# A product-key expert layer: three instead of two token blocks by gathered rows, one-hots made four tokens at a time, expert names resolved in batches

## Chip, cores and metric

One core of a Trainium2 chip. The metric is the device time of one execution in microseconds (us), median of several runs. The engines are TensorE (PE; its weight loads are PEld), VectorE (DVE), ScalarE (ACT), GpSimd (POOL) and SyncE (SP, here only a DMA queue).

## The reference

A decoder layer on 1024 tokens of width 1024. Its first half (projections, retention and window attention, layer norm) is untouched by the change. The second is an expert FFN whose experts are single neurons:

```python
q = (xt @ w_pq).reshape(T, 8, 2, 128)
s = einsum('thpd,hpkd->thpk', q, sub_keys)            # 2 x 128 scores per head
s1, i1 = top_k(s[:, :, 0], 16); s2, i2 = top_k(s[:, :, 1], 16)
cand = s1[..., :, None] + s2[..., None, :]            # 256 pairs
top_s, pos = top_k(cand, 16)                          # idx = i1 * 128 + i2 of the pair
g = softmax(top_s)                                    # 8 heads x 16 experts a token
a = gelu(x . u_tab[idx]) * g                          # 16384 experts in all
y = sum over the 128 chosen of a * v_tab[idx]
h = layer_norm(ALPHA * h + y)
```

## The kernel before

Five stages follow one another, each a block that all engines leave together: `project`, `attend`, `score`, `experts_in` and `experts_out`. Tokens lie in TB = 8 blocks of 128.

**Two ways to the same sum.** For the first GB = 2 token blocks each chosen row is gathered: an indirect DMA on GpSimd's queue fetches for 128 tokens one row of 1024 numbers each (512 KB), 128 gathers a block. For the other DB = 6 blocks all 16384 experts are computed densely (DT = 768 tokens), as 128 slices of 128 experts, and a matrix of gates, zero where an expert isn't chosen, selects.

**`score`** computes scores head by head (a turn for each of PH = 8 heads) and stores those of blocks 1 to 7. Beside it VectorE does the top-k of token block 0: `side` twice (top 16 of 128), `pairs` (top 16 of 256), `gaps`, and, one turn later, `names` (which expert each of the 16 places means, by a compare with 0..15, a product and a sum) and `gates` (the softmax), which needs `exp` of ScalarE.

**`experts_in`** runs eight blocks s = 0..7 of four turns q; a turn has eight steps n, numbered m = 4s + q. In each step TensorE does half an expert slice: z = u . h for half of the dense tokens, 24 matmuls (three for each of eight pieces of the width, the operands being split in a high and a low part, `u_hi` by ScalarE, `u_lo` by GpSimd, line 787). ScalarE copies z out and stores it. From s = GB on, TensorE also builds the gates matrix of token block s: four matmuls a step, one for each token, of two one-hot matrices, `hot2` (line 1211) and `hot1_g` (line 1213, one-hot times gate). VectorE's order in a step is `make_hot`, a piece of the top-k of token block s + 1 (piece n % 4: two sides, pairs, names), and one `dot` (line 1222) of a gathered row of u with the token's own h, from a ring of four row buffers. GpSimd's order in a step is `u_lo` (every second step) and one gather, which waits until its ring slot is used. TensorE, in order, does a half slice, then waits for the one-hots of the step before. The semaphores are `hot_in` (one-hots ready), `row_here` and `row_used` (ring), `z_done`, `u_hi_in`, `u_lo_in`.

**`experts_out`** runs NG = 32 rounds of four slices over the dense token blocks. Each step of a round is one token block: ScalarE's gelu, VectorE's product with the gates (line 1442), ScalarE's `a_hi`, VectorE's `a_lo` (line 1447), 24 matmuls of 512 columns with v (lines 1346 to 1348), and VectorE's two additions of the sums to y (line 1455). Between these VectorE adds gathered rows of v to y for the gathered blocks (`add_row`, line 1434), 256 in all over the first 31 rounds, again through a ring of four (`RING`); `added` frees a slot. GpSimd splits v (`v_lo`, line 1397, four a round, each behind ScalarE's `v_hi`) and issues the gathers between (line 1387). `finish` is the last layer norm of a token block.

Of the kernel before, what the change touches and what calls it, by code (L numbers as in the profile page):

```python
# [33 lines left out]
GB = 2  # L34
# [213 lines left out]
class Ahead:  # L248
# [5 lines left out]
    def __init__(self, nc, ctx):  # L254
# [4 lines left out]
        self.g_in = self.carve(DT // GT, GROUP * GT)  # L259
        self.v_raw = [self.carve(D) for _ in range(2)]  # L260
# [5 lines left out]
        self.wq_raw = [self.carve(KT, P) for _ in range(2)]  # L266
        self.wq_here = [sem(f"wq_here{p}") for p in range(2)]
# [432 lines left out]
class TopK:  # L700


    def __init__(self, nc, ctx):
        sb = memory(nc, ctx)[0]
        self.nc = nc
        self.places = sb("places", [P, TOPK])
        self.s_cp, self.s_left = sb("s_cp", [P, 2, NK]), sb("s_left", [P, 2, NK])
        self.top, self.top_f = sb("top", [P, 2, TOPK]), sb("top_f", [P, 2, TOPK])
        self.top_i = sb("top_i", [P, 2, TOPK], U32)
        self.cand, self.cand_left = sb("cand", [P, TOPK, TOPK]), sb("cand_left", [P, TOPK * TOPK])  # L710
        self.best, self.pos = sb("best", [P, TOPK]), sb("pos", [P, TOPK], U32)
        self.ab, self.ab_f = sb("ab", [P, 2, TOPK], U32), sb("ab_f", [P, 2, TOPK])
        self.pick = sb("pick", [P, 2, TOPK, TOPK])
        self.gap, self.gap_e = sb("gap", [P, TOPK]), sb("gap_e", [P, TOPK])
        self.gap_sum, self.gap_r = sb("gap_sum", [P, 1]), sb("gap_r", [P, 1])
        self.found = sb("found", [P, 3, PH, TOPK])
# [10 lines left out]
    def side(self, link, p):  # L727

        self.top16(link, self.s_cp[:, p], self.s_left[:, p], self.top[:, p], self.top_i[:, p])

    def pairs(self, link):
# [3 lines left out]
        self.top16(link, self.cand[:].rearrange("p a b -> p (a b)"), self.cand_left[:], self.best, self.pos)  # L735

    def gaps(self):

        return self.nc.vector.tensor_scalar(self.gap[:], self.best[:], self.best[:, 0:1], None, ALU.subtract)

    def names(self, link, h):
# [3 lines left out]
        nc.vector.tensor_copy(self.top_f[:], self.top_i[:])  # L745
        nc.vector.tensor_scalar(self.ab[:, 0], self.pos[:], 4, None, ALU.logical_shift_right)
        link(nc.vector.tensor_scalar(self.ab[:, 1], self.pos[:], 15, None, ALU.bitwise_and))
        link(nc.vector.tensor_copy(self.ab_f[:], self.ab[:]))
        link(nc.vector.tensor_tensor(self.pick[:], bc(self.ab_f[:], 3, TOPK),
                                     bc(bc(self.places[:], 1, TOPK), 1, 2), ALU.is_equal))  # L750
        link(nc.vector.tensor_tensor(self.pick[:], self.pick[:], bc(self.top_f[:], 2, TOPK), ALU.mult))
        link(nc.vector.tensor_reduce(self.found[:, 0:2, bass.ds(h, 1), :].rearrange("p a h k -> p a (h k)"),
                                     self.pick[:], AX.X, ALU.add))

    def exp(self):

        return self.nc.scalar.activation(self.gap_e[:], self.gap[:], ACT.Exp, accum_out=self.gap_sum[:])

    def gates(self, link, h):
        nc = self.nc  # L760
        link(nc.vector.reciprocal(self.gap_r[:], self.gap_sum[:]))
        link(nc.vector.tensor_scalar(self.found[:, 2, bass.ds(h, 1), :].rearrange("p h k -> p (h k)"),
                                     self.gap_e[:], self.gap_r[:], None, ALU.mult))
# [27 lines left out]
def score(nc, d, hT_hi, hT_lo, tk, tiles, ahead):  # L791
# [3 lines left out]
    with ExitStack() as ctx:  # L795
# [18 lines left out]
        with nc.Block() as block:  # L814
# [56 lines left out]
            def _(act):  # L871
# [17 lines left out]
                def turn(h):  # L889
                    last = isinstance(h, int) and h == PH - 1  # L890
                    query(h, 0)
                    if not (isinstance(h, int) and h == 0):
                        act.wait_ge(gaps, h)
                        tk.exp().then_inc(exps, 1)
# [18 lines left out]
                act.wait_ge(gaps, PH)  # L913
# [9 lines left out]
            def _(v):  # L923
# [18 lines left out]
                def finish_top(h):  # L942

                    tk.names(link, h)
                    v.wait_ge(exps, h + 1)
                    tk.gates(link, h)

                def turn(h):
                    last = isinstance(h, int) and h == PH - 1
# [3 lines left out]
                    if not (isinstance(h, int) and h == 0):  # L953
                        finish_top(h - 1)
# [8 lines left out]
                    tk.side(link, 0)  # L963
                    tk.side(link, 1)
                    tk.pairs(link)
                    tk.gaps().then_inc(gaps, 1)
# [5 lines left out]
                turns(v, PH, turn)  # L972
                finish_top(PH - 1)


def experts_in(nc, d, hT_hi, hT_lo, tk, tiles, ahead):
# [7 lines left out]
    RING = 4  # L984
    PER_TURN = GB * PH * TOPK // TB
    with ExitStack() as ctx:
# [6 lines left out]
        hot2 = [sb(f"hot2_{g}", [P, 4, NK]) for g in range(2)]  # L993
        hot1_g = [sb(f"hot1_g{g}", [P, 4, NK]) for g in range(2)]
        g_sb = [sb(f"g_sb{b}", [P, NK, GT]) for b in range(2)]
        rows_in = ahead.rows + [sb(f"u_rows{i}", [P, D]) for i in range(RING - len(ahead.rows))]
        h_own = sb("h_own", [P, GB, D])
        z_ps = [[bank(f"z_ps{e}{a}") for a in range(2)] for e in range(2)]
        g_ps = [ctx.enter_context(nc.psum_tensor(f"g_ps{g}", [P, 4, NK], F32)) for g in range(2)]
        product = ctx.enter_context(nc.psum_tensor("product", [P, D], F32))  # L1000
# [8 lines left out]
        hot_in = [sem(f"hot_in{g}") for g in range(2)]  # L1009
        g_done = [sem(f"g_done{g}") for g in range(2)]  # L1010
# [564 lines left out]
```

## Time and profile before

| | |
|---|---|
| median of 3 runs | 3459.11 us (3454.69 to 3463.78) |
| the profiled execution | 3475.62 us, span 3474.0 us |
| busy in the span: PE, DVE, ACT, POOL | 3085.9, 2711.0, 987.2, 1418.4 us |
| mean granted clock of TensorE | 0.953 |
| `project`, `attend`, `score` | 0 to 747.8 us |
| `experts_in` | 747.8 to 2321 us |
| handing over | 2321 to 2366 us |
| `experts_out` | 2366 to 3474 us |

Busy is time in which an engine executes; waits don't count. A window of the span divides this by stage, and the difference between its length and an engine's busy time is that engine's idle time. Instructions of one engine overlap at their ends, so the distance between two starts, not the length, is what one costs. An instruction that is held up by another engine's use of memory is shown as a long one, not as idle time.

### The profile page before, as it was taken

What the parts mean: (1) busy time and instruction counts of PE and PEld (TensorE: products, weight loads), DVE (VectorE), ACT (ScalarE), POOL (GpSimd) and SP (SyncE); (2) the same over time, 40 slices, a digit from 0 to 9 for tenths busy, and PEclk for the clock granted to TensorE, in tenths of its full rate; (3) what the DMA queues carried; (4) which work ended last, traced back from release to release, by engine and by line L of the source; (5) the groups of instructions that cost most, each with busy time, mean ns of one, the idle gap of its engine ahead of it and who ended that gap; (6) DMA issues with size and microseconds to landing.
All of it is one profiled execution on the core that took longest, in us unless ns stands there. A gap on an engine that the chain in (4) does not pass through costs nothing. (4 is left out here: it accounts for less than half of the span.)

```text
span 3474.0 us, 43072 instructions
## 1 busy us (share of the span) xinstructions
PE 3085.9 (89%) x15866; PEld 2757.8 (79%) x15866; DVE 2711.0 (78%) x5430; ACT 987.2 (28%) x1565; POOL 1418.4 (41%) x878
## 2 busy tenths in 40 slices
PE   8997989989987888888888888866999999999997
PEld 6886877879887888787878888865787888787886
DVE  4125764559999989989899897546888898888889
ACT  2103331112222332333323333332332333333331
POOL 4113210025543333333333333335665656566563
PEclk9998999999998999999999999988999999999999
DMA  4214222336654554554555545658888788787873
GB/s 163 98 61 151 90 72 82 98 115 210 217 206 174 202 191 177 202 204 174 214 190 188 207 176 208 228 193 284 298 283 302 266 284 289 266 296 270 295 272 115
DMA packets 294042, 695.59 MB, mean 200 GB/s; under 512 B 20448, under 2 KB 136544, under 8 KB 290656
## 3 DMA queue, kind: packets, MB, share of 16 engines
q1 hardware_dynamic: 190944, 316.66, 27.8%
q0 software_dynamic: 73728, 268.47, 20.9%
q10 hardware_dynamic: 29184, 108.01, 7.9%
q8 instruction: 113, 1.85, 0.2%
q14 instruction: 73, 0.60, 0.0%
HBM read 565.13 MB, written 127.93 MB: 200 GB/s over the span
## 5 line engine op out<-in xcount | busy, mean ns | idle before, releaser
L787 POOL TENSOR_TENSOR u_lo<-u_raw,u_hi 128x1024 fp32r<-128x1024 f32 x128 | 321.6, 2512 | 1116.9 <-ACT u_hi L783 1116.7
L1062 PE MATMUL z_ps<-hT_hi,u_hi 128*128 128x384 f32 x2048 | 728.0, 355 | 35.2 <-POOL u_lo L787 23.8
L1063 PE MATMUL z_ps<-hT_lo,u_hi 128*128 128x384 f32 x2048 | 709.2, 346 | 0.0
L1064 PE MATMUL z_ps<-hT_hi,u_lo 128*128 128x384 f32 x2048 | 707.4, 345 | 0.0
L1346 PE MATMUL y_ps<-v_hi,a_hi 128*128 128x512 f32 x1536 | 603.8, 393 | 70.4 <-DVE a_lo L1447 45.0
L1347 PE MATMUL y_ps<-v_lo,a_hi 128*128 128x512 f32 x1536 | 601.2, 391 | 0.0
L1348 PE MATMUL y_ps<-v_hi,a_lo 128*128 128x512 f32 x1536 | 600.7, 391 | 0.0
L1397 POOL TENSOR_TENSOR v_lo<-room,v_hi 128x1024 fp32r<-128x1024 f32 x128 | 344.2, 2690 | 248.8 <-ACT v_hi L1374 247.1
L1062 PEld LDWEIGHTS z_ps<-hT_hi,u_hi 128*128 128x128 f32 x2048 | 406.4, 198 | 39.6 <-POOL u_lo L787 28.0
L1072 PE MATMUL g_ps<-hot_g,hot 128*128 128x128 f32 x1536 | 232.9, 299 | 193.8 <-DVE hot_g L1213 193.8
L1063 PEld LDWEIGHTS z_ps<-hT_lo,u_hi 128*128 128x128 f32 x2048 | 404.8, 198 | 0.0
L1064 PEld LDWEIGHTS z_ps<-hT_hi,u_lo 128*128 128x128 f32 x2048 | 403.0, 197 | 0.0
L1346 PEld LDWEIGHTS y_ps<-v_hi,a_hi 128*128 128x128 f32 x1536 | 290.1, 189 | 142.1 <-DVE a_lo L1447 45.2
L1072 PEld LDWEIGHTS g_ps<-hot_g,hot 128*128 128x128 f32 x1536 | 210.4, 207 | 219.9 <-DVE hot_g L1213 219.9
L1348 PEld LDWEIGHTS y_ps<-v_hi,a_lo 128*128 128x128 f32 x1536 | 290.4, 189 | 61.0
L1347 PEld LDWEIGHTS y_ps<-v_lo,a_hi 128*128 128x128 f32 x1536 | 290.3, 189 | 59.6
L1129 ACT ACTIVATE z_sb<-z_ps 128x384 f32<-128x384 f32 x256 | 124.7, 490 | 700.5 <-PE z_ps L1064 700.5
L1213 DVE TENSOR_SCALAR hot_g<-iota,iT,gT 128x128 f32<-128x128 f32 x768 | 320.5, 482 | 0.0
L1434 DVE SCALAR_TENSOR_TENSOR y<-v_rows,a_rows,y 128x1024 f32<-128x1024 f32 x192 | 277.8, 1468 | 29.0 <-DMA v_rows<-in_v,room 28.9
L1387 POOL DMA_INDIRECT v_rows<-in_v,room x192 | 238.7, 1243 | 135.2 <-DVE y L1434 102.4
L1115 ACT ACTIVATE g_sb<-g_ps 128x512 f32<-128x512 f32 x192 | 212.3, 1106 | 261.1 <-PE g_ps L1072 261.1
L1222 DVE CUSTOM_DVE_ANT_0 product<-u_rows,h_own 128x1024 f32<-128x1024 f32 x192 | 244.7, 1274 | 40.0 <-DMA u_rows<-in_u,room 35.4
(184 smaller groups left out, 5010.4 us busy)
## 6 DMA issues: line engine op xcount, KB each, us to landing
u_raw<-in_uT SPq DMA_DIRECT2D x128, 512.0 KB, 3.6
room<-in_v SPq DMA_DIRECT2D x128, 512.0 KB, 6.7
z<-z_sb ACTq DMA_DIRECT2D x128, 384.0 KB, 2.6
gates<-g_sb ACTq DMA_DIRECT2D x24, 2048.0 KB, 7.9
z_in<-z SPq DMA_DIRECT2D x16, 1536.0 KB, 12.7
g_in<-gates SPq DMA_DIRECT2D x16, 1536.0 KB, 19.5
room<-z SPq DMA_DIRECT2D x15, 1536.0 KB, 12.2
room<-gates SPq DMA_DIRECT2D x15, 1536.0 KB, 20.3
```

Source lines behind the costliest of these rows:

```text
L787: self.nc.gpsimd.tensor_tensor(self.u_lo[e][:], self.u_raw[e][:], self.u_hi[e][:].bitcast(F32), ALU.subtract).then_inc(self.u_lo_in[e], 1)
L1062: nc.tensor.matmul(o, u_hi[e][:, k], hT_hi[:, k, cols], start=(k == 0), stop=False)
L1063: nc.tensor.matmul(o, u_hi[e][:, k], hT_lo[:, k, cols], start=False, stop=False)
L1064: last = nc.tensor.matmul(o, u_lo[e][:, k], hT_hi[:, k, cols], start=False, stop=(k == KT - 1))
L1072: last = nc.tensor.matmul(g_ps[g][:, t], hot2[g][:, t], hot1_g[g][:, t], start=True, stop=True)
L1213: last = nc.vector.tensor_scalar(hot1_g[g][:, t], iota[:], iT[:, 0, t0 + t:t0 + t + 1], gT[:, t0 + t:t0 + t + 1], ALU.is_equal, ALU.mult)
L1222: nc.vector.tensor_tensor_reduce(product[:], rows_in[r][:], h_own[:, b], 1.0, 0.0, ALU.mult, ALU.add, ahead.z_rows[:, b, slot:slot + 1]).t ...
L1346: nc.tensor.matmul(o, ah, v_hi[p][:, i, c], start=(i == 0), stop=False)
L1347: nc.tensor.matmul(o, ah, v_lo[p][:, i, c], start=False, stop=False)
L1348: last = nc.tensor.matmul(o, al, v_hi[p][:, i, c], start=False, stop=(i == GROUP - 1))
L1397: nc.gpsimd.tensor_tensor(v_lo[r % 2][:, i], v_raw[i % 2][:], v_hi[r % 2][:, i].bitcast(F32), ALU.subtract).then_inc(v_lo_in[i % 2], 1)
L1434: nc.vector.scalar_tensor_tensor(y[:, b], rows_in[i % RING][:], a_rows[:, b, slot:slot + 1], y[:, b], ALU.mult, ALU.add).then_inc(added[b], 1)
```

## The change

GB goes from 2 to 3: 384 instead of 256 rows are gathered in either expert stage, the dense part has 5 token blocks (640 tokens, matmuls of 320 columns in `experts_in`, five steps a round in `experts_out`), and the gates matrix begins at s = 3. In `experts_in` dots are spread unevenly over the blocks, the ring has three slots, and h is loaded a token block at a time into two buffers. Both one-hots are plain compares for four tokens at once, with 0..127 read from a copy in PSUM (`iota_ps`); ScalarE multiplies one of them by the gates. `names` and `gates` are no longer done head by head, but for four and for eight heads; the top-k reads the loaded scores without a copy. The out stage's code is unchanged but for GB.

```diff
-GB = 2
+GB = 3
@@ class TopK
-    def names(self, link, h):
+    def names(self, link, half):
         nc = self.nc
-        nc.vector.tensor_copy(self.top_f[:], self.top_i[:])
...
-        link(nc.vector.tensor_copy(self.ab_f[:], self.ab[:]))
...
+        hs = slice(half * PH // 2, (half + 1) * PH // 2)
+        nc.vector.tensor_scalar(self.ab[:, 0], self.pos[:, hs], 4, None, ALU.logical_shift_right)
+        link(nc.vector.tensor_scalar(self.ab[:, 1], self.pos[:, hs], 15, None, ALU.bitwise_and))
+        link(nc.vector.tensor_tensor(self.pick[:], bc(self.ab[:].rearrange("p a h k -> p a (h k)"), 3, TOPK),
+                                     bc(bc(self.places[:], 1, PH // 2 * TOPK), 1, 2), ALU.is_equal))
+        for a in range(2):
+            last = nc.vector.tensor_tensor(...)
+        link(last)
+        link(nc.vector.tensor_reduce(...))
@@ score, VectorE: behind the last head
-                turns(v, PH, turn)
-                finish_top(PH - 1)
+                for h in range(PH):
+                    turn(h)
+                tk.gaps().then_inc(gaps, 1)
+                for half in range(2):
+                    tk.names(link, half)
+                v.wait_ge(exps, 1)
+                tk.gates(link)
@@ experts_in
-    RING = 4
-    PER_TURN = GB * PH * TOPK // TB
+    RING = 3
+    PER_TURN = [48, 48, 48, 46, 46, 46, 46, 56]
...
+        def own_rows(s, q, n):
+            before, k = sum(PER_TURN[:s]), q * 8 + n
+            return range(before + PER_TURN[s] * k // 32, before + PER_TURN[s] * (k + 1) // 32)
@@ SyncE
-                sp.dma_start(h_own[:], d["h"].rearrange("n p c -> p n c")[:, 0:GB]).then_inc(h_here, 16)
+                for b in range(2):
+                    sp.dma_start(h_own[b][:], d["h"][b]).then_inc(h_here[b], 16)
                 for m in range(Q * TB):
+                    done = own_rows(m // Q, m % Q, 0).start // (PH * TOPK)
+                    if done > (...) and done + 1 < GB:
+                        sp.wait_ge(row_used, done * PH * TOPK)
+                        sp.dma_start(h_own[(done + 1) % 2][:], d["h"][done + 1]).then_inc(...)
@@ ScalarE
+                def scale_hot(gm, n):
+                    g, t0 = n % 2, gm % Q * GT + 4 * n
+                    act.wait_ge(hot_in[g], 4 * gm + n // 2 + 1)
+                    for t in range(4):
+                        last = nc.scalar.activation(hot1_g[g][:, t], hot1[g][:, t], ACT.Copy,
+                                                    scale=gT[:, t0 + t:t0 + t + 1])
+                    last.then_inc(hot_g_in[g], 1)
...
                             if s >= GB:
+                                scale_hot(gm, n)
                                 if n:
                                     take_gates(gm, n - 1)
@@ GpSimd
-                            gather(s * PER_TURN + q * 8 + n)
+                            for i in own_rows(s, q, n):
+                                gather(i)
@@ VectorE
+                link(nc.vector.tensor_copy(iota_ps, iota[:]))
...
+                def top_piece(s, q, n):
+                    m, j, piece = s * Q + q, n // 3, n % 3
+                    if j < 2:
...
+                    elif n == 6 and q % 2:
+                        tk.names(link, q // 2)
+                    elif n == 7 and q == Q - 1:
+                        v.wait_ge(exps, s + 1)
+                        tk.gates(link)
...
-                    nc.vector.tensor_tensor(hot2[g][:], bc(iota[:], 1, 4), bc(iT[:, 1, t0:t0 + 4], 2, NK), ALU.is_equal)
-                    for t in range(4):
-                        last = nc.vector.tensor_scalar(hot1_g[g][:, t], iota[:], iT[:, 0, t0 + t:t0 + t + 1],
-                                                       gT[:, t0 + t:t0 + t + 1], ALU.is_equal, ALU.mult)
+                    for hot, side in ((hot2, 1), (hot1, 0)):
+                        last = nc.vector.tensor_tensor(hot[g][:], bc(iota_ps, 1, 4), bc(iT[:, side, t0:t0 + 4], 2, NK),
+                                                       ALU.is_equal)
...
-                            dot(s * PER_TURN + q * 8 + n)
+                            for i in own_rows(s, q, n):
+                                dot(i)
```

VectorE's order in one step of `experts_in` where both kinds of work run (names: `hot` a one-hot, `room`, `u_rows` row buffers, `near` the PSUM copy of 0..127; ISA rows with h_own are the dots), before:

```order
L1211 TENSOR_TENSOR hot_0<-iota,iT 128x512
L1213 TENSOR_SCALAR hot_g<-iota,iT,gT 128x128 x4
L734 TENSOR_TENSOR cand<-top 128x256
L721 MAX best<-cand 128x8
L722 MAX_INDEX pos<-best,cand 128x8
L723 MATCH_REPLACE cand_left<-best,cand 128x256
L724 MAX best<-cand_left 128x8
L725 MAX_INDEX pos<-best,cand_left 128x8
L739 TENSOR_SCALAR gap<-best 128x16
L1222 ISA product,room<-u_rows,h_own 128x1024
```

and now:

```order
L1242 TENSOR_TENSOR hot_0<-near,iT 128x512 x2
L738 TENSOR_TENSOR room<-top 128x256
L725 MAX best<-room 128x8
L726 MAX_INDEX pos<-best,room 128x8
L727 MATCH_REPLACE room<-best,room 128x256
L728 MAX best<-room 128x8
L729 MAX_INDEX pos<-best,room 128x8
L1253 ISA u_rows,room<-u_rows,h_own 128x1024
L1253 ISA room 128x1
L1253 ISA room<-room,h_own 128x1024
```

Five one-hot instructions have become two, and every second step has a second dot.

GpSimd's order in a round of `experts_out` (gathers into `v_rows` or, for one ring slot, `room`), before:

```order
L1397 TENSOR_TENSOR v_lo<-room,v_hi 128x1024
L1387 DMA v_rows<-in_v,room 128x1024 x2
L1397 TENSOR_TENSOR v_lo<-room,v_hi 128x1024
L1387 DMA v_rows<-in_v,room 128x1024
L1387 DMA room<-in_v,room 128x1024
L1387 DMA v_rows<-in_v,room 128x1024
L1397 TENSOR_TENSOR v_lo<-room,v_hi 128x1024
L1387 DMA v_rows<-in_v,room 128x1024 x2
```

and now:

```order
L1429 TENSOR_TENSOR v_lo<-room,v_hi 128x1024
L1419 DMA v_rows<-in_v,room 128x1024
L1419 DMA room<-in_v,room 128x1024
L1419 DMA v_rows<-in_v,room 128x1024
L1429 TENSOR_TENSOR v_lo<-room,v_hi 128x1024
L1419 DMA v_rows<-in_v,room 128x1024 x2
L1419 DMA room<-in_v,room 128x1024
L1419 DMA v_rows<-in_v,room 128x1024
L1429 TENSOR_TENSOR v_lo<-room,v_hi 128x1024
```

Mostly two gathers stood between two splits of v; now there are three or four.

## Rows read from the trace of the kernel before

**Rows 1.** Windows by stage: us, busy (x count) per engine, granted clock, DMA share, GB/s.

```profile
747.80:913.00 165.20, 153.93 (x845) 152.04 (x846) 148.29 (x356) 36.51 (x69) 87.75 (x53) 0.96 0.65 221
913.00:1066.60 153.60, 130.28 (x721) 127.72 (x720) 146.38 (x355) 30.94 (x61) 76.58 (x47) 0.95 0.60 207
1066.60:1279.00 212.40, 181.97 (x1028) 178.30 (x1027) 193.58 (x514) 66.28 (x96) 73.66 (x47) 0.91 0.49 178
2131.40:2321.00 189.60, 166.37 (x996) 163.87 (x996) 111.66 (x226) 60.90 (x77) 71.16 (x45) 0.95 0.59 220
2401.00:3401.00 1000.00, 979.01 (x4268) 801.95 (x4267) 868.96 (x957) 324.10 (x472) 614.97 (x360) 0.99 0.83 285
```

**Rows 2.** VectorE by line, 1066.6 to 2131.4: count, busy us, mean ns, idle before it.

```profile
L1213 DVE TENSOR_SCALAR hot_g<-iota,iT,gT 128x128 f32<-128x128 f32 x640 | 276.7, 497 | 0.0
L1211 DVE TENSOR_TENSOR hot<-iota,iT 128x512 f32<-128x512 f32 x160 | 157.9, 987 | 0.2
...
L1222 DVE CUSTOM_DVE_ANT_0 product<-room,h_own 128x1024 f32<-128x1024 f32 x40 | 49.3, 1233 | 43.7 <-issue 42.9
```

**Rows 3.** VectorE's timeline in block 3: start us, length us, instruction.

```profile
1291.71 1.23 DVE L1222 CUSTOM_DVE_ANT_0 product<-u_rows,h_own 128x1024 f32<-128x1024 f32 x1
...
1292.87 0.69 DVE L1211 TENSOR_TENSOR hot<-iota,iT 128x512 f32<-128x512 f32 x1
1293.47 1.11 DVE L1213 TENSOR_SCALAR hot_g<-iota,iT,gT 128x128 f32<-128x128 f32 x4
1294.50 0.42 DVE L734 TENSOR_TENSOR cand<-top 128x256 f32<-128x256 f32 x1
```

**Rows 4.** VectorE by line, 747.8 to 1066.6 (blocks 0 and 1).

```profile
L762 DVE TENSOR_SCALAR found<-gap_e,gap_r 128x16 f32<-128x16 f32 x16 | 37.0, 2314 | 0.6
L748 DVE CAST ab_f<-ab 128x32 f32<-128x32 uint32 x16 | 31.2, 1948 | 0.5
```

**Rows 5.** VectorE's timeline at the end of the scoring stage, last head.

```profile
737.09 0.28 DVE L961 TENSOR_SCALAR s_cp<-s_out 128x256 f32<-128x256 f32 x1
737.42 0.29 DVE L721 MAX8 top<-s_cp 128x8 f32<-128x128 f32 x1
...
743.86 0.23 DVE L739 TENSOR_SCALAR gap<-best 128x16 f32<-128x16 f32 x1
...
746.95 0.23 DVE L762 TENSOR_SCALAR found<-gap_e,gap_r 128x16 f32<-128x16 f32 x1
```

**Rows 6.** VectorE by line, 2401 to 3401 (out rounds).

```profile
L1434 DVE SCALAR_TENSOR_TENSOR y<-v_rows,a_rows,y 128x1024 f32<-128x1024 f32 x184 | 265.6, 1465 | 20.6 <-DMA v_rows<-in_v,room 20.5
...
L1447 DVE TENSOR_TENSOR a_lo<-room,a_hi 128x512 fp32r<-128x512 f32 x89 | 105.7, 1187 | 0.0
...
L1434 DVE SCALAR_TENSOR_TENSOR y<-room,a_rows,y 128x1024 f32<-128x1024 f32 x61 | 85.0, 1393 | 110.4 <-DMA room<-in_v,room 110.4
```

**Rows 7.** VectorE's timeline, one step of an out round.

```profile
2723.05 1.27 DVE L1455 TENSOR_TENSOR y<-y_ps,y 128x512 f32<-128x512 f32 x2
2724.25 0.67 DVE L1447 TENSOR_TENSOR a_lo<-room,a_hi 128x512 fp32r<-128x512 f32 x1
2724.85 1.27 DVE L1434 SCALAR_TENSOR_TENSOR y<-v_rows,a_rows,y 128x1024 f32<-128x1024 f32 x1
2726.05 0.67 DVE L1442 TENSOR_TENSOR room<-room 128x512 f32<-128x512 f32 x1
```

**Rows 8.** Source view of line 1455: ns min/median/max, first and last start.

```profile
L1455 DVE TENSOR_TENSOR y<-y_ps,y x384: 668/676/687, 2386.9 to 3465.4; 128x512 f32<-128x512 f32 x192
```

**Rows 9.** VectorE by line, 2131.4 to 2321 (block 7).

```profile
L1222 DVE CUSTOM_DVE_ANT_0 product<-room,h_own 128x1024 f32<-128x1024 f32 x8 | 11.3, 1412 | 51.0 <-DMA room<-in_u,room 51.0
```

**Rows 10.** TensorE's timeline in an out round.

```profile
2724.39 0.39 PE L1346 MATMUL y_ps<-v_hi,a_hi 128*128 128x512 f32 x1
2724.62 0.39 PE L1347 MATMUL y_ps<-v_lo,a_hi 128*128 128x512 f32 x1
```

**Rows 11.** DMA issues, 2401 to 3401: count, median us to landing.

```profile
v_rows<-in_v,room POOLq DMA_INDIRECT x183, 8.2
```

More of the change, by code:

```diff
@@ L700, with __init__ @@
 class TopK:
-    def __init__(self, nc, ctx):
+    def __init__(self, nc, ctx, room):
         sb = memory(nc, ctx)[0]
@@ L940, in scores @@
                                           s_ps[p][1][:].rearrange("p (t k) -> p t k", k=NK)).then_inc(s_dve, 1)
[L942 to L946, printed above, removed]
                 def turn(h):
-                    last = isinstance(h, int) and h == PH - 1
+                    last = h == PH - 1
                     query(h, 0)
@@ L962, in turn @@
                     nc.vector.engine_nop().then_inc(s_taken, 1)
[L963 to L966, printed above, removed]
+                    for p in range(2):
+                        tk.side(link, p, h, tk.s_cp[:, p])
+                    tk.pairs(link, h)
                     chain.restart()
@@ L993, in experts_in @@
         hot2 = [sb(f"hot2_{g}", [P, 4, NK]) for g in range(2)]
+        hot1 = [sb(f"hot1_{g}", [P, 4, NK]) for g in range(2)]
         hot1_g = [sb(f"hot1_g{g}", [P, 4, NK]) for g in range(2)]
@@ L996, in experts_in @@
         rows_in = ahead.rows + [sb(f"u_rows{i}", [P, D]) for i in range(RING - len(ahead.rows))]
-        h_own = sb("h_own", [P, GB, D])
+        h_own = [sb(f"h_own{b}", [P, D]) for b in range(2)]
         z_ps = [[bank(f"z_ps{e}{a}") for a in range(2)] for e in range(2)]
         g_ps = [ctx.enter_context(nc.psum_tensor(f"g_ps{g}", [P, 4, NK], F32)) for g in range(2)]
-        product = ctx.enter_context(nc.psum_tensor("product", [P, D], F32))
+        near = ctx.enter_context(nc.psum_tensor("near", [P, 512], F32))
+        iota_ps, iT_ps, gT_ps = near[:, 0:NK], near[:, P:3 * P].rearrange("p (a t) -> p a t", a=2), near[:, 3 * P:]
         const_here, u_here, u_hi_in, u_lo_in = tiles.const_here, tiles.u_here, tiles.u_hi_in, tiles.u_lo_in
@@ L1009, in experts_in @@
         hot_in = [sem(f"hot_in{g}") for g in range(2)]
+        hot_g_in = [sem(f"hot_g_in{g}") for g in range(2)]
         g_done = [sem(f"g_done{g}") for g in range(2)]
@@ L1012, in experts_in @@
         g_stored = [sem(f"g_stored{b}") for b in range(2)]
-        picked_in, h_here = sem("picked_in"), sem("h_own_here")
+        picked_in, h_here = sem("picked_in"), [sem(f"h_own_here{b}") for b in range(2)]
         row_here = [sem(f"u_row_here{i}") for i in range(RING)]
@@ L1491, in build @@
             attend(nc, d, hT_hi, hT_lo, ahead, spent)
-            tk = TopK(nc, inner)
+            tk = TopK(nc, inner, ahead)
             tiles = ExpertTiles(nc, inner)
```

100 lines of the change are left out of this document (49 added, 51 removed).

## The prediction

> **What bounds the kernel now.** I read the windows first, stage by stage, then the costs by line inside them, then the timeline for the distance from one start to the next. The "in" stage is eight blocks of 16 expert slices. Blocks 0 and 1 take 165 and 154 us, blocks 2 to 6 take 212 to 213 us each (five alike, the first stands there), block 7 takes 190 us; then come 32 "out" rounds, of which a stretch of 1000 us is shown [rows 1]. The reader is to see which engine is full: VectorE is busy 148 of 165, 146 of 154 and 194 of 212 us, and the granted clock there is 0.91 to 0.96, so TensorE, though busy, pauses. In the out rounds TensorE is busy 979 of 1000 us. So the in stage is paced by VectorE (block 7 less clearly, 112 of 190) and the out stage by TensorE.
>
> The second thing to see is how much of VectorE's time is a standstill. In blocks 2 to 6 the group of one-hot instructions on line 1213 has a mean of 497 ns and line 1211 of 987 [rows 2], while the same instructions undisturbed start 0.60 (line 1211) and 1.03 us for all four (line 1213) before the next [rows 3]. Over five blocks, 640 x (497-340) + 160 x (987-690) ns is 148 us (340 for one of the four: 1.11 less three starts of 0.257), 30 us a block; with 44 us of unexplained idle before the dots [rows 2] that is about 40 us a block. In blocks 0 and 1 it is line 762 (2314 ns for 16 elements, 230 elsewhere) and the cast of line 748 (1948 ns for 32 elements), together about 31 us a block [rows 4, 5].
>
> **Change, part 1: the end of the scoring stage.** Per head, the two sides and the pairs run from 737.42 to 743.86, 6.4 us, and the names and gates until 747.18, 3.3 us [rows 5]. The latter now leaves the turns, where TensorE hides it, and comes once behind the last head, where nothing hides it since all engines wait for the block's end. Price of a batched piece: 512 elements take 0.67 us and 1024 take 1.27 [rows 7], so 1.15 ns an element and about 2.45 us for 2048. One half is two shifts (0.3), a compare (2.45), two products of 1024 (2.5) and a sum (2.45): 7.7 us. Two halves are 15.4, plus 0.9 for the gates, against 3.3 now: **+13 us**.
>
> **Part 2: blocks 0 to 2 (no gates matrix now in block 2 either).** VectorE per block, undisturbed: top-k 8 x 6.4 = 51 plus 15.4 + 1.3 = 67 us (now 8 x 10.1 = 81), and 48 dots of 1.16 us [rows 3] = 56 us (now 37). That is 123 us against 118. On top there are about 41 us of standstill now. The two worst offenders shrink from eight times a block to a few, but more dots stand beside the same 16 u_lo instructions; I keep 31 (bounds 10 and 45). 154 us a block. TensorE needs less than now, since each matmul has 320 columns for 384; ScalarE and GpSimd are far from full. Three blocks: 462 against 165 + 154 + 212 = 531, **-69 us**.
>
> **Part 3: blocks 3 to 6.** One-hots: two compares of 0.60 us for 32 turns = 38 us, for 32 x 1.63 = 52 now. Top-k 67 for 81. Dots 46 x 1.16 = 53 for 37. Sum 158.5 against 170. The real gain is the standstill of 43 us: the 30 us that lie in the one-hots should go, because their first operand now lies in PSUM. The nearest row is the addition of line 1455, of the same size with one operand in PSUM: 384 of them lie between 668 and 687 ns [rows 8], while line 1447, of the same size with both in SBUF, has a mean of 1187 beside the same GpSimd work [rows 6]. The Trainium skill, SBUF — State Buffer, section "Who interferes with whom", has this as a rule: VectorE and GpSimd share one port pair as an exclusive lock, and an instruction with at most one SBUF input outside the two-port modes does not contend. By that rule, the trace agrees. I leave 17 us around the 46 dots and 4 us of waits for the transposes: 180 us (bounds 167, with hardly any standstill, and 202, with all of it). ScalarE gets four scalings a turn; at the 0.26 us of one of VectorE's [rows 3] that is 33 us on top of 66 of 212 [rows 1]: off the path. What is moved: SP's load of h_own is split in three with one wait for row_used ahead of it, in front of u loads that are needed a turn later; I cost it at nothing. Four blocks: **-132 us**.
>
> **Part 4: block 7.** No top-k, but 56 dots for 32. Here VectorE is idle 78 us, almost all of it in front of dots: 51 us for one ring slot alone [rows 9]. The order explains it: a gather stands behind u_lo on GpSimd's queue, this waits for u_hi on ScalarE, this for matmuls, and these for one-hots that stand behind the dot. The loop gets 0.4 us a turn shorter by the one-hots and longer by the scaling and a second dot. I take 176 for 190, **-14 us** (bounds 155 and 200).
>
> In stage in all: **-215 us**.
>
> **Part 5: the out rounds.** Matmuls start 0.23 us apart [rows 10], 979/4268 = 0.229 in the stretch [rows 1]: 144 a round are 33.0 us, 120 are 27.5. If TensorE stayed the bound, 32 rounds would give back 176 us. VectorE decides against it. 245 row additions in 1000 us at 256/31 = 8.26 a round make a round of 33.7 us; VectorE is busy 869 and the remaining 131 us are all waits for a gathered row [rows 1, 6]. Starts inside one undisturbed step: two additions 1.20, a_lo 0.60, row 1.20 us [rows 7]. With the mean stretch of rows 6 (rows 1.447 against 1.27, a_lo 1.187 against 0.68) a round now has 8.26 x 1.38 = 11.4, 12 x 0.60 = 7.2, 6 x 1.11 = 6.7, and the remainder of the 29.3 busy, 4.0, for six products. After: 384/31 = 12.39 rows x 1.38 = 17.1, 10 additions 6.0, 5 a_lo 5.5, 5 products 3.3: 31.9 us busy, above TensorE's 27.5. The waits for rows are 4.4 us a round now, and slack, since TensorE is full; once VectorE is the bound they are on the path. Do they go away? A slot comes free with its addition, and the gather into it takes 8.2 us to land [rows 11]; four slots at 12.39 rows in T us need a turnaround of T/3.1. At T = 36.7 that is 11.8 us: 8.2 to land, 1.2 the addition, and 2.4 us for GpSimd, which may be in a v_lo of 2.4 us or waiting for v_hi with the gathers behind it, and for VectorE's other steps. I take waits of 4.8 us, T = 36.7 (bounds 31.9, no waits, and 41). 31 rounds x 3.0 = +93, the last round, without rows, -6: **+87 us**.
>
> **Sum:** 13 - 69 - 132 - 14 + 87 = -115 us. On the profiled execution, 3475.6, that is 3361; it lay 16 us over the median of 3459.1, so the forecast is **3344 us**.
>
> **Rivals.**
> 1. *Rows land in time.* The gathers are issued early enough and only the 31.9 us stay: 31 x (-1.8) - 6 = -62 in place of +87, so 3195 us. For it: once TensorE has time to spare, ScalarE's v_hi and GpSimd's v_lo come earlier, and the gathers behind them. Against it: turnaround would have to be 10.3 us, hardly more than landing plus addition. 14%.
> 2. *The ring decides (slower than before).* One mechanism in the out rounds: four slots, three rows for each v_lo, and each slot's cycle is 8.2 + 1.2 + 3.8 = 13.2 us, a round of 13.2 x 3.1 = 40.9, +223 - 6. The same in the in stage, where the ring shrinks to three: 10.5 us a cycle is 3.5 a row, 168 a block in blocks 0 to 2 (-27) and 196 in block 7 (+6), blocks 3 to 6 unchanged. Sum 13 - 27 - 132 + 6 + 217 = +77: 3536 us. It makes the kernel slower from about 12.4 us on in the out stage, if the in stage suffers too, and from 13 if not. For it: the waits are there already, with 8.26 rows. Against: now the gathers also wait because TensorE is slow. 14%.
> 3. *The one-hots still stand still* (the change doesn't do what it should): the 30 us stay in blocks 3 to 6 and most in block 7, +145: 3489 us. Line 1455 speaks against it. 6%.
>
> Another is inside the forecast: TensorE, with 27 us of work in a round of 37, pauses in each step. In block 2, at 182 us busy in 212, the granted clock was still 0.91 [rows 1]; only under 0.75 would the matmuls need the whole round. The Trainium skill, TensorE: Matmul & The Clock Gate, Part 1, has the engine fall to 1.2 GHz after idling; were that so throughout, 54 us a round would be needed and the kernel far slower. The row of the in blocks says pauses of this kind cost a tenth.
>
> **How the numbers follow.** Forecast 66%, rivals 14, 14 and 6. A measurement of this kernel can tell about 0.3%, 10 us, from no change. Faster: nearly all of the forecast and rival 1, 0.79. Slower: most of rivals 2 and 3, 0.16. Within 0.3%: what of each falls about the old time, 0.05. The range 3220 to 3500 takes in the forecast's bounds (in stage -260 to -130, out stage +20 to +160, not all at one end), rival 3 and the nearer halves of rivals 1 and 2.
>
> **What would show it.** VectorE's one-hots near 0.68 us without a tail; blocks 3 to 6 at about 180 us, blocks 0 to 2 at about 154; the in stage beginning some 13 us later behind the last scores; TensorE's busy share in the out rounds about 75% with VectorE's idle time all before row additions; a round of about 36.7 us. I am wrong if rounds get shorter than 33 us or longer than 40, or if blocks 3 to 6 stay above 200.

## The result and the profile after

The changed kernel takes **3862.45 us** (median of 4 runs, 3857.36 to 3866.29) against 3459.48 (4 runs, 3454.69 to 3463.78): a ratio of 1.1164, 95% interval 1.1144 to 1.1185. That is 403 us slower where 115 us less were forecast, and far outside the range. The profiled span is 3855.6 us, the mean granted clock 0.867 (before 3474.0 and 0.953).

First the stages: blocks 0, 1 and 2, then a stretch of one block's length among blocks 3 to 6, block 7 with the end of the stage, and 1140 us of out rounds, as in [rows 1]. This is the windows view of the changed kernel; columns are the stretch, its length, then the busy time (and number) of PE, PEld, VectorE, ScalarE and GpSimd, the granted clock, the DMA share and GB/s.

```profile
761.00:935.00 174.00, 143.08 (x862) 139.95 (x863) 142.73 (x317) 34.31 (x54) 106.57 (x67) 0.91 0.74 248
935.00:1101.40 166.40, 128.89 (x763) 125.21 (x763) 146.07 (x314) 31.01 (x49) 104.00 (x65) 0.90 0.73 240
1101.40:1276.70 175.30, 117.05 (x711) 113.48 (x710) 143.21 (x316) 28.85 (x46) 102.02 (x65) 0.87 0.70 230
1535.00:1800.00 265.00, 171.08 (x1026) 166.26 (x1026) 163.70 (x374) 96.89 (x209) 92.82 (x64) 0.81 0.51 179
2320.40:2563.00 242.60, 168.90 (x1000) 164.69 (x998) 106.06 (x177) 94.57 (x206) 90.87 (x71) 0.83 0.62 220
2640.00:3780.00 1140.00, 880.88 (x3530) 708.37 (x3529) 1016.39 (x959) 284.44 (x412) 783.50 (x485) 0.87 0.86 293
```

In the fourth row no engine is full. VectorE is busy 163.7 of 265 us, close to the 158.5 that the prediction added up, and the block lasts 265 all the same. TensorE is busy 171. With no engine full and the DMA share down at 0.51, waits must set the pace, and one looks for a chain of waits that comes back to its start, a circle.

Measured between the same marks in both kernels, in us. The in stage starts with its first matmul; blocks are divided where VectorE starts on a block (block 0 is counted from the start of the stage, block 7 to its last matmul); an out round is the time from the first row addition to the last, divided by 31:

| | in stage starts | blocks 0, 1, 2 | blocks 3 to 6 | block 7 | out round |
|---|---|---|---|---|---|
| before | 747.9 | 165 154 213 | 215 212 211 214 | 188 | 33.5 |
| forecast | +13 | 154 154 154 | 180 each | 176 | 36.7 |
| after | 761.0 | 174 167 175 | 258 265 260 260 | 236 | 38.2 |

By spans: +13 before the in stage, +229 in it (1802.0 for 1573.2), -4 in the handing over, +143 in the out stage (1251.6 for 1108): 381.

The waits of blocks 3 to 6 in the changed kernel name the links of the circle (columns: who waited, for whom, us in total, how often, longest).

```profile
POOL u_lo L794 <- ACT u_hi L790: 630.6, 64, 12.9
ACT hot_g L1129 <- DVE hot L1242: 555.7, 116, 17.3
...
PE g_ps L1087 <- ACT hot_g L1129: 352.6, 76, 10.2
DVE u_rows L1253 <- issue: 132.8, 23, 10.0
DVE u_rows L1253 <- DMA u_rows<-in_u,room: 123.8, 30, 7.6
```

GpSimd waits 631 of 1043 us for u_hi, 64 times, which is every time, and ScalarE 556 us for one-hots. The first of these alone shows nothing new: in blocks 3 to 6 of the kernel before (852 us) it was there as well, with the same count and nearly the same share of the time:

```profile
POOL u_lo L787 <- ACT u_hi L783: 522.2, 64, 12.8
```

There ScalarE waited for TensorE (361 us for z, 181 for the gates matrix) and 47 us for VectorE's gaps, never for one-hots. Its wait for VectorE's one-hots is the new link. One turn of the circle, in the timeline of the changed kernel in block 4 (start, duration, engine, line, operation, in brackets the idle time before it):

```profile
1597.76 1.06 ACT L790 ACTIVATE u_hi<-u_raw 128x1024 fp32r<-128x1024 f32 x1
...
1598.90 2.39 POOL L794 TENSOR_TENSOR u_lo<-u_raw,u_hi 128x1024 fp32r<-128x1024 f32 x1 [12.38 <-ACT u_hi L790]
...
1601.44 0.96 POOL L1188 DMA_INDIRECT room<-in_u,room  x1
...
1602.29 1.27 ACT L1129 ACTIVATE hot_g<-hot,gT 128x128 f32<-128x128 f32 x4
...
1607.22 1.23 DVE L1253 CUSTOM_DVE_ANT_0 room<-room,h_own 128x1024 f32<-128x1024 f32 x1 [9.88 <-issue]
...
1608.37 1.28 DVE L1242 TENSOR_TENSOR hot<-near,iT 128x512 f32<-128x512 f32 x2
...
1609.69 0.40 ACT L1129 ACTIVATE hot_g<-hot,gT 128x128 f32<-128x128 f32 x1 [3.78 <-DVE hot L1242]
...
1610.87 1.06 ACT L1139 ACTIVATE g_sb<-g_ps 128x512 f32<-128x512 f32 x1
...
1611.71 1.07 ACT L790 ACTIVATE u_hi<-u_raw 128x1024 fp32r<-128x1024 f32 x1
```

The circle runs from u_hi to GpSimd's u_lo; behind it on GpSimd's queue stands the gather, 5.8 us before its dot starts; behind the dot on VectorE's queue come the next step's one-hots; ScalarE's scaling waits for these, and behind the scaling on ScalarE's queue stands the next u_hi. From u_hi to u_hi is 13.95 us here; a block has 16 of them, and its 260 us make 16.2 us for the mean one. Before, what ScalarE waited for in a step was `take_gates`, the result of one-hots that are a step older, so the same circle had a step of slack.

In the out stage the two costs to compare with [rows 6] are these (VectorE's lines in the stretch of 1140 us; busy, mean ns of one, idle before and its releaser):

```profile
L1466 DVE SCALAR_TENSOR_TENSOR y<-v_rows,a_rows,y 128x1024 f32<-128x1024 f32 x276 | 457.3, 1675 | 86.5 <-DMA v_rows<-in_v,room 86.3
...
L1466 DVE SCALAR_TENSOR_TENSOR y<-room,a_rows,y 128x1024 f32<-128x1024 f32 x91 | 139.8, 1536 | 40.0 <-DMA room<-in_v,room 40.0
L1479 DVE TENSOR_TENSOR a_lo<-z_in,a_hi 128x512 fp32r<-128x512 f32 x75 | 94.7, 1263 | 0.0
```

### The profile page after: what moved, and what is told of

Its sections match the earlier page's. It is cut to its first block and busy times, and to the rows that moved or that the text cites. A ratio compares the mean times of both kernels' runs of the same rounds, so it can differ in the third digit from the quotient of the medians.

```text
span 3855.6 us, 40781 instructions
## 1 busy us (share of the span) xinstructions
PE 2884.6 (75%) x14839; PEld 2559.1 (66%) x14839; DVE 2672.7 (69%) x4479; ACT 1058.1 (27%) x1989; POOL 1748.9 (45%) x1134
## 5 line engine op out<-in xcount | busy, mean ns | idle before, releaser
L1077 PE MATMUL z_ps<-hT_hi,u_hi 128*128 128x320 f32 x2048 | 707.9, 346 | 135.0 <-POOL u_lo L794 110.8
L1078 PE MATMUL z_ps<-hT_lo,u_hi 128*128 128x320 f32 x2048 | 682.8, 333 | 0.0
L1079 PE MATMUL z_ps<-hT_hi,u_lo 128*128 128x320 f32 x2048 | 679.6, 332 | 0.0
L1253 DVE CUSTOM_DVE_ANT_0 u_rows<-u_rows,h_own 128x1024 f32<-128x1024 f32 x256 | 326.3, 1275 | 389.0 <-DMA u_rows<-in_u,room 240.0
L1466 DVE SCALAR_TENSOR_TENSOR y<-v_rows,a_rows,y 128x1024 f32<-128x1024 f32 x288 | 480.4, 1686 | 89.3 <-DMA v_rows<-in_v,room 89.1
L1380 PE MATMUL y_ps<-v_hi,a_lo 128*128 128x512 f32 x1280 | 524.0, 409 | 0.0
L1419 POOL DMA_INDIRECT v_rows<-in_v,room x288 | 367.4, 1276 | 215.4 <-DVE y L1466 160.0
L1129 ACT ACTIVATE hot_g<-hot,gT 128x128 f32<-128x128 f32 x640 | 204.5, 390 | 668.8 <-DVE hot L1242 668.8
L1188 POOL DMA_INDIRECT u_rows<-in_u,room x256 | 300.8, 1175 | 162.2 <-DVE room L1253 107.2
L1253 DVE CUSTOM_DVE_ANT_0 room<-room,h_own 128x1024 f32<-128x1024 f32 x128 | 220.9, 1726 | 173.7 <-DMA room<-in_u,room 99.9
```

The source lines that it names most:

```text
L1077: nc.tensor.matmul(o, u_hi[e][:, k], hT_hi[:, k, cols], start=(k == 0), stop=False)
L1078: nc.tensor.matmul(o, u_hi[e][:, k], hT_lo[:, k, cols], start=False, stop=False)
L1079: last = nc.tensor.matmul(o, u_lo[e][:, k], hT_hi[:, k, cols], start=False, stop=(k == KT - 1))
L1253: nc.vector.tensor_tensor_reduce(rows_in[r][:], rows_in[r][:], h_own[b % 2][:], 1.0, 0.0, ALU.mult, ALU.add, ahead.z_rows[:, b, slot:slot ...
L1380: last = nc.tensor.matmul(o, al, v_hi[p][:, i, c], start=False, stop=(i == GROUP - 1))
L1419: nc.gpsimd.indirect_dma_start(out=rows_in[i % RING][:], out_offset=None, in_=d["v"].rearrange("a b c -> (a b) c"), in_offset=bass.Indirec ...
```

## The experiments

The time of the kernel before, on the same chips, is 3457.5 beside the first four kernels, 3463.4 beside the next four and 3463.7 (median of 9) beside the last four. All but e11 are single runs. Most differences read from them are of tens of us; those of a few us are taken from parts of one trace beside parts of another and are worth less.

**e1: u_hi ahead of the scaling.** ScalarE makes the next u_hi as soon as the second half of an expert slice is copied out, ahead of the scaling of that step instead of behind it.

```diff
+                split_u(0, 1)
...
-                            if a == 0 and 4 * m + n // 2 < NK - 1:
-                                split_u(m, n // 2 + 1)
...
                                 act.dma_start(d["z"][4 * m + 2 * j + e], z_sb[e][:]).then_inc(z_stored[e], 16)
+                                if 4 * m + n // 2 + 1 < NK - 1:
+                                    split_u(m + (n == 7), (n // 2 + 1) % 4 + 1)
```

> The changed kernel, but on ScalarE's queue the split of the next expert slice (u_hi) stands ahead of the scaling of the one-hots and not behind it; nothing else differs. Theory (a circle through queues): u_hi stands behind the scaling, this behind VectorE's one-hots, these behind a dot, this behind a gather, this behind u_lo on GpSimd, and this behind u_hi: 1.1 + 2.4 + 5.8 + 1.2 + 1.2 + 1.3 + 1.1 us and what they are held up make the 16 us that two steps take (260 us a block). With u_hi ahead the circle has another step of slack: blocks 3 to 6 fall to 185 to 210 us, block 7 to 175 to 200, the whole by 200 to 300 us. Rival (ring): three slots for half as many rows again set the pace; then blocks 3 to 6 stay at 250 to 265 us. Blocks 0 to 2 have no one-hots and stay at 166 to 175 us by both; the out stage stays at 1250 us.

3627.9 us. Blocks 3 to 7 take 213, 215, 215, 215 and 190 us, 231 less in all, and nothing else moves (blocks 0 to 2: 174, 166, 177; round 38.3). The order of one instruction on one queue is worth nearly all of the 239 us that blocks 3 to 7 had lost against the kernel before. The blocks stay a little above the 185 to 210 us expected. Windows of this kernel, a stretch of one block's length:

```profile
1535.00:1750.00 215.00, 160.41 (x1027) 157.96 (x1027) 168.55 (x374) 100.81 (x209) 94.67 (x62) 0.86 0.65 221
```

Still no engine is full. The same order was not tried in the kernel before, so it isn't known how much of the gain that kernel would have had too; e2 takes away the new link alone.

**e2: the one-hots as before, no scaling on ScalarE.** Undoes the other half of the link.

```diff
-                                scale_hot(gm, n)
...
-                    for hot, side in ((hot2, 1), (hot1, 0)):
-                        last = nc.vector.tensor_tensor(hot[g][:], bc(iota_ps, 1, 4), ...)
+                    nc.vector.tensor_tensor(hot2[g][:], bc(iota[:], 1, 4), ...)
+                    for t in range(4):
+                        last = nc.vector.tensor_scalar(hot1_g[g][:, t], iota[:], ..., ALU.is_equal, ALU.mult)
```

> The changed kernel with the one-hots made as before: one compare for four tokens, then four compare-and-scale instructions on VectorE, no scaling on ScalarE; three gathered blocks and the batched names stay. Theory (circle through ScalarE's queue): the circle is cut here too, but the standstill beside GpSimd returns, about 30 us a block, and the one-hots cost 52 for 38 us: blocks 3 to 6 at 205 to 230 us. Rival (ring): they stay at 255 us or more, since the one-hots even cost more.

3703.5 us, blocks 3 to 6 at 229. Without the scaling the blocks are 32 us shorter than in the changed kernel, though VectorE is now busier: 192 of 229 us, for 164 of 265 in the changed kernel and 169 of 215 in e1.

**e3: a ring of four in the in stage** (`RING = 3` to `RING = 4` in `experts_in`).

> The changed kernel with four row buffers for u in place of three. Theory (circle): blocks 3 to 6 stay within 5 us of 260; only blocks 0 to 2, where GpSimd waits 166 us for a slot and TensorE behind it 111 us for u_lo, fall from 166-175 to 150-160 us. Rival (ring): blocks 3 to 6 fall too, by a fifth to a quarter, to 200 to 215 us.

3828.7 us. Blocks 3 to 7 are unchanged (261 265 260 260 238): a free slot is not what they wait for. Blocks 0 to 2 become 160, 151 and 164, 40 us less together. There the ring of three does cost, 13 us a block.

**e4: the changed kernel with two gathered blocks** (`GB = 2`, `PER_TURN = [32] * 8`), the rest of the change kept.

> The changed kernel with two gathered token blocks as before (32 dots a block of the in stage, matmuls of 384 columns, six steps an out round); one-hots, scaling, batched names and the ring of three stay. Theory (circle): what the circle holds hardly depends on how many rows there are, so blocks 2 to 6 take 230 to 260 us against 213 before; blocks 0 and 1 take 140 to 160; the out stage is back at 1108 us (it has nothing else of the change); the whole is 3500 to 3650 us. Rival (rows): with 32 dots for 46 the in stage is at or under the time before, blocks 2 to 6 at 213 us or less, the whole at or under 3460. In either case the out stage shows that its own loss of 143 us comes from the third block alone.

3575.9 us. Blocks 2 to 6 take 232 to 236 us, some 20 more than in the kernel before, with VectorE busy 145 of 232: the circle holds with a single dot a step as well. But it is shorter: blocks 3 to 7 take 1154 us together for 1279 in the changed kernel, so of the 48 us that a block had lost, about half come with the third gathered block, whose dots and gathers lie in the circle. The theory had the circle hardly depend on the number of rows, and this half it missed. The out round is back at 33.1, so there the third block costs some 160 us.

**e5: e1, and on GpSimd the gathers of two steps ahead of the next u_lo.**

```diff
-                        for n in range(8):
-                            if n % 2 == 0 and 4 * m + n // 2 < NK - 1:
-                                split_u(m, n // 2 + 1)
-                            for i in own_rows(s, q, n):
+                        for n in range(0, 8, 2):
+                            for i in (*own_rows(s, q, n), *own_rows(s, q, n + 1)):
                                 gather(i)
+                            if 4 * m + n // 2 < NK - 1:
+                                split_u(m, n // 2 + 1)
```

> The kernel of e1 (u_hi ahead of the scaling) with GpSimd's queue turned round: the two or three gathers of a pair of steps stand ahead of its u_lo instead of behind it. Theory (circle): what is left of the circle in e1 (215 us a block) is the stretch from u_hi by u_lo to the gather, 3.5 us; a gather that doesn't wait for it lands before its dot, so blocks 3 to 6 fall to 175 to 200 us and block 7 to 165 to 180. Rival (VectorE is simply full, or the ring of three is): blocks 3 to 6 stay at 210 us or more. Blocks 0 to 2 may get worse, since u_lo now waits for ring slots.

3536.2 us: blocks 3 to 6 at 194 to 198, block 7 at 175. Here the forecast's way of counting, by VectorE's work, holds. Windows of this kernel, a stretch of one block's length:

```profile
1500.00:1695.00 195.00, 154.00 (x1036) 151.28 (x1035) 179.86 (x377) 101.11 (x210) 96.24 (x64) 0.89 0.72 243
```

VectorE is busy 179.9 of 195 us: the block is paced by it. The forecast had 176 us of work and standstill and 4 of waits; here the waits are 15.

**e6: e1 with a ring of six in the out stage** (`RING = 4` to `6` in `experts_out`).

> The kernel of e1 with six row buffers for v in place of four, in the out stage alone. There a round takes 38.3 us; VectorE is busy 34.4 of them and waits 4.3 for rows, GpSimd is busy 26.5 and waits 7.7 for ring slots, with v_lo, and TensorE for that, behind these waits. Theory (ring): with six slots both waits go, and the round falls to VectorE's busy time, 34 to 35.5 us, 90 to 130 us in all. Rival (transfers): the 16 DMA engines, busy 86% in this stage, only let rows land later with more of them under way; the round stays above 37 us. Rival (VectorE held up by GpSimd): GpSimd, no longer waiting, holds VectorE up more; the round stays above 36.5 us with VectorE busy over 36.

3621.4 us, a round of 37.7 for 38.3. More slots alone bring 0.6 us a round; the theory's 34 to 35.5 missed. The waits of its out rounds (2440 to 3500 us) show why:

```profile
POOL v_lo L1430 <- ACT v_hi L1407: 200.8, 28, 9.3
...
DVE y L1467 <- DMA v_rows<-in_v,room: 65.9, 48, 7.0
DVE y L1467 <- DMA room<-in_v,room: 57.8, 24, 7.3
```

GpSimd's wait for slots has gone from 226 of 1140 us in the changed kernel to 43 of 1060. But the gathers stand on its queue behind a v_lo that waits for v_hi, and the waits for rows stay (124 us of 1060).

**e7: e4 with e1's edit**, and **e8: e4 with e1's and e5's edits and a ring of four in the in stage.**

> The kernel of e4 (two gathered blocks, everything else of the change) with u_hi ahead of the scaling. Theory (circle): blocks 2 to 6 fall from 234 to 185 to 205 us, block 7 from 219 to 180 to 190; the rest as in e4, so the whole is 3370 to 3440 us, faster than the kernel before. Rival: TensorE's 384 columns and lower clock hold blocks 2 to 6 above 213 us and the whole at or over 3460.

> The kernel of e7 with the gathers ahead of u_lo and a ring of four for u. Theory (circle): blocks 2 to 6 come to TensorE's own time, 165 to 185 us, block 7 to 165 to 180, blocks 0 and 1 to 135 to 150, the whole to 3230 to 3330 us. Rival: the gathers in front make u_lo, and with it TensorE, wait for ring slots; blocks 2 to 6 stay over 195 us.

3402.0 and 3273.8 us, both inside what the circle's theory expected (one block of e7, at 213, lies above its 205). Blocks 3 to 7 of e7 take 205, 204, 201, 213 and 183; those of e8 184 four times and 166, with blocks 0 and 1 at 142 and 134 and an out round of 33.3.

**e9: e1 with the low part of v nearly left out.** In `experts_out` v_lo is computed for 64 of 1024 columns from the third round on, so that part of the dense product is left out; it measures what GpSimd's subtraction costs VectorE.

```diff
-                        nc.gpsimd.tensor_tensor(v_lo[r % 2][:, i], v_raw[i % 2][:], ...
+                        wd = D if r < 2 else 64
+                        nc.gpsimd.tensor_tensor(v_lo[r % 2][:, i, 0:wd], v_raw[i % 2][:, 0:wd], ...
```

> The kernel of e1, but from the third out round on GpSimd computes only 64 of the 1024 columns of each v_lo (the low part of v is left out of the sums for the other columns, so this part of the computation is missing); all instructions, waits and transfers stay. It takes away most of the 9.6 us a round in which GpSimd's v_lo can hold VectorE up. Theory (hold-up): row additions are stretched by 0.38 us each and a_lo by 0.5, 7 us a round; this goes, rows are back at 1.27 to 1.35 us, GpSimd has time, and the round falls from 38.3 to 29 to 33 us. Rival (landing): the rows' 8 us to land and the four slots set the pace; the round stays above 36 us with VectorE waiting for rows longer than now.

The round falls to 33.9 us. VectorE's lines in 900 us of its out rounds:

```profile
L1469 DVE SCALAR_TENSOR_TENSOR y<-v_rows,a_rows,y 128x1024 f32<-128x1024 f32 x247 | 315.0, 1290 | 93.6 <-DMA v_rows<-in_v,room 93.3
...
L1469 DVE SCALAR_TENSOR_TENSOR y<-room,a_rows,y 128x1024 f32<-128x1024 f32 x83 | 106.6, 1284 | 74.9 <-DMA room<-in_v,room 74.7
```

A row addition into y from `v_rows` takes 1290 ns for 1675: the stretch comes from GpSimd's subtraction. VectorE's busy time falls from 34.3 to 27.5 us a round (731.5 of 900). Yet the waits for rows grow to 168 of 900 us, 6.3 a round, with the DMA share at 0.94. So the round came out above the theory's 29 to 33 us and under the rival's 36.

**e10: e6, and the gathers of a round's first share ahead of its first v_lo.**

```diff
+                        mid = mine[len(mine) * i // GROUP:len(mine) * (i + 1) // GROUP]
+                        if i == 0:
+                            for k in mid:
+                                gather(k)
                         pool.wait_ge(v_hi_in[i % 2], 2 * r + i // 2 + 1)
...
-                        for k in mine[len(mine) * i // GROUP:len(mine) * (i + 1) // GROUP]:
+                        for k in mid if i else ():
```

> The kernel of e6 (six slots for v) with the gathers behind each round's first v_lo moved ahead of it, so that at a round's end they no longer stand behind v_hi of the next round (GpSimd waits 200 us for v_hi in e6, VectorE 124 us for rows). Theory (queue order): VectorE's waits for rows fall from 4.4 to under 2 us a round, and the round from 37.7 to 34.5 to 36. Rival (transfers late anyway, or the hold-up grows by as much as the waits shrink): the round stays above 37 us.

3521.1 us, a round of 34.7. VectorE's lines in 900 us, then the windows of the same stretch:

```profile
L1471 DVE SCALAR_TENSOR_TENSOR y<-v_rows,a_rows,y 128x1024 f32<-128x1024 f32 x267 | 487.0, 1860 | 5.4 <-DMA v_rows<-in_v,room 5.4
...
L1471 DVE SCALAR_TENSOR_TENSOR y<-room,a_rows,y 128x1024 f32<-128x1024 f32 x53 | 76.6, 1446 | 0.4 <-DMA room<-in_v,room 0.4
```

```profile
2440.00:3340.00 900.00, 758.95 (x3062) 603.56 (x3061) 894.19 (x836) 245.26 (x359) 743.19 (x422) 0.94 0.91 322
```

The waits for rows are gone (5.8 of 900), as the theory said, and VectorE is full, 894 of 900. But GpSimd now works 83% of the time instead of 70, and the additions from `v_rows` stretch to 1860 ns (all 320 together from 1.67 us in e6 to 1.79). Of the 4.4 us of waits a round in e6, 1.2 are given back so (busy 33.3 a round there, 34.5 here).

**e12: everything mended with three gathered blocks** (e5, a ring of four in the in stage, e10's out stage), beside **e11: the kernel of e8 again**, with five executions, on the same chip.

> Three gathered blocks with every order mended: e5 and four slots for u, six for v and the order of e10. It differs from e8 by the third block and the out stage's ring and order. Theory (VectorE has no room for a third block): blocks 3 to 6 at 185 to 197 us against 184 in e8, the out round at 34.5 to 37.5 us against 33.3, the whole 3400 to 3500 us, slower than e8 by over 100 us. Rival (only the queues were in the way): with TensorE's work smaller by a sixth it is at or under e8, 3280 us or less.

> The kernel of e8 again, timed against the kernel before: two gathered blocks, compares and scaling split between VectorE and ScalarE, batched names, u_hi ahead of the scaling, gathers ahead of u_lo, four slots. Expected ratio 0.940 to 0.952 of the kernel before.

e12 takes 3323.95 us. e11 takes **3275.71** (3268.24 to 3283.72), a ratio of 0.9465 to the kernel before, interval 0.9445 to 0.9485. The windows of e11 in blocks 3 to 6 and in the out rounds, then of e12 in blocks 3 to 6:

```profile
1300.00:1484.00 184.00, 170.13 (x1026) 169.34 (x1026) 150.67 (x346) 103.41 (x209) 80.24 (x49) 0.94 0.63 223
2400.00:3200.00 800.00, 795.36 (x3495) 654.65 (x3494) 713.24 (x779) 268.03 (x388) 495.44 (x290) 1.00 0.83 286
```

```profile
1460.00:1648.00 188.00, 153.99 (x1025) 151.02 (x1023) 172.63 (x371) 99.10 (x207) 95.48 (x63) 0.90 0.74 250
```

In e11 TensorE is busy 170 of 184 and 795 of 800 us, at a granted clock of 0.94 and 1.00: that kernel is paced by TensorE in both. With three blocks TensorE has a sixth less to do, and still the blocks take 188 and the rounds 34.5, with VectorE busy 172.6 of 188 us and TensorE only 154. The third block costs 48 us, with all orders mended; the out stage of e11 keeps four slots and the old order, which with TensorE busy 795 of 800 us there can cost it little. Blocks and rounds of e12 lie in the ranges of the first theory, but its time, 48 us over e11, lies between the two theories' numbers.

## Why the prediction was wrong

Against its own sum the profiled execution is about 495 us too long: 324 in blocks 3 to 6, 60 in block 7, 54 in blocks 0 to 2, 56 in the out stage, none at the end of the scoring stage.

**Part 1 was right.** The in stage starts 13.1 us later. Timeline of the changed kernel, VectorE behind the last head:

```profile
744.54 0.29 DVE L743 TENSOR_TENSOR gap<-best 128x128 f32<-128x128 f32 x1 [0.21 <-DVE pos L729]
...
745.07 2.29 DVE L752 TENSOR_TENSOR room<-ab,places 128x2048 f32<-128x2048 uint32 x1
747.40 2.36 DVE L755 TENSOR_TENSOR room<-room,top_i 128x1024 f32<-128x1024 f32 x2
749.79 2.29 DVE L759 TENSOR_REDUCE found<-room 128x128 f32<-128x2048 f32 x1
```

2.29 and 2.36 us for 2.45 and 2.5: the price by the element was good to 7%.

**Part 2 failed by the ring.** 516 us for 462. The ring of three costs 40 of these 54 (e3). The prediction named that only in rival 2, at 168 us a block; 174, 167 and 175 were measured. What the other 14 are was not tried.

**Part 3 is the step that failed.** Its sentence was: "ScalarE gets four scalings a turn; at the 0.26 us of one of VectorE's [rows 3] that is 33 us on top of 66 of 212 [rows 1]: off the path." ScalarE's busy time was counted rightly enough (96.9 of 265 us; 1.27 us for the four, at 1602.29 in the timeline above, for 1.04). What failed is "off the path": the place of the scaling in ScalarE's queue was not looked at. The scaling brings a wait for VectorE, and behind that wait stands u_hi, for which GpSimd, the gathers, the dots and in the end the same one-hots wait. The prediction had described this circle in part 4, for block 7, and changed it there by fractions of a microsecond; it did not ask in part 3 whether the new wait takes a step of slack out of it. So blocks 3 to 6 took 258 to 265 us for 180. e1 takes the link away by order (213 to 215 us) and e2 by undoing it (229); by e3 the ring has no part in it, and by e4 the circle is there without the third block (232 to 236), which adds about 26 us a block to it. With the second link, u_lo ahead of the gathers, gone too (e5), the blocks take 194 to 198, inside the bounds of 167 and 202. What was said of the one-hots themselves held (VectorE's lines of the changed kernel, blocks 3 to 6, then the source view of the same line, with the shortest, median and longest in ns):

```profile
L1242 DVE TENSOR_TENSOR hot<-near,iT 128x512 f32<-128x512 f32 x256 | 164.3, 683 | 0.1
```

```profile
L1242 DVE TENSOR_TENSOR hot<-near,iT x256: 672/681/692, 1277.4 to 2311.9; 128x512 f32<-128x512 f32 x128
```

All 256 of them lie between 672 and 692 ns: no tail. Rival 3 is out, and the rule of the Trainium skill, SBUF — State Buffer, section "Who interferes with whom", that an instruction with at most one SBUF input does not contend with GpSimd, agrees with this row.

**Part 4** fell with part 3: 236 us for the forecast's 176. In e5, where the circle is broken, block 7 takes 175.

**Part 5 had the right mechanism and one term mis-sized.** VectorE sets the round and its idle time lies before row additions (126 us in 1140, 4.3 a round, for 4.8); TensorE is busy 77% (forecast 75). But VectorE's busy time is 34.3 us a round (1016.4 over 29.6 rounds), not 31.9. The failing term is the stretch taken over from [rows 6]: rows 1.64 us by mean (276 at 1675 and 91 at 1536) for 1.447, which is 12.39 x 0.19 = 2.4 us. In the traces 60 of 244 row additions overlap a v_lo before and 113 of 366 after; these take 1.98 and 2.46 us by mean, all others 1.27 and 1.28. So a quarter met GpSimd's subtraction before and three tenths now, and a meeting costs more, which is the larger part of the difference. Why it costs more was not tried. 31 rounds of 38.2 us for 33.5 are +146, and +143 was measured for the forecast's +87. Rival 1 is out. Rival 2, the ring, gave 0.6 us a round by itself in the out stage (e6) and is part of the truth in blocks 0 to 2. That the waits for rows came out near the 4.8 us is in part luck: with six slots they stayed at 4.4 a round, and only the order of the gathers took them away (e10, which had six slots as well; the order with four was not tried).

**The clock.** In blocks 3 to 6 the mean granted clock is 0.81, where TensorE works 171 of 265 us with pauses, and 0.87 in the out rounds; between full speed (2.4 GHz) and half (1.2 GHz) that is about 62 and 74% of the time at full. It did not fall to half throughout, and with TensorE busy two thirds of the time it was not the limit. In blocks 3 to 6 it was higher where the gaps were shorter: 0.86 in e1, 0.89 in e5, 0.94 in e11, where TensorE has 384 columns for 320 to do.

## What to carry to other kernels

When work moves to an engine with time to spare, list what stands behind its new wait on that in-order queue, and follow those to the instruction that the wait is for: if the list comes back to it, the length of that circle can set the time, whatever the busy times say. A producer that others wait for (here u_hi) belongs ahead of such a wait. And an engine's mean durations hold for the mix they were measured in; put on the path beside a busier neighbour, they can grow, as the row additions did.

## What the runs showed of the hardware

- A row addition with its operands in SBUF takes, by the mean of all, 1.29 us with GpSimd's subtraction nearly gone (e9), 1.45 before (GpSimd busy 61% of the time), 1.64 after (69%) and 1.79 in e10 (83%): here, removing waits of one engine lengthened another's instructions.
- Four scalings of 128 x 128 with a scale for each partition take ScalarE 1.27 us, started 0.3 us apart, though one of them has a mean of 390 ns.
- The landing of a gather of 128 rows of 4 KB took longer where the DMA engines were fuller, but from a share of 0.83 on it grew no more. In the timeline of block 4 above, at a share of 0.51, it takes at most 5.8 us. In the out rounds it is 8.2 us before, at 0.83 [rows 11], 7.7 after, at 0.86 (the line below, from the transfers' view: the count, then the median from issue to landing), and 7.8 and 8.2 by buffer in e9, at 0.94.

```profile
v_rows<-in_v,room POOLq DMA_INDIRECT x275, 7.7
```
